# Sliding-window attention on one Trainium2 core: the next head's projection, cut in 32 pieces, is spread otherwise over the stages of a head

## The reference, cut to what matters

```
q = rope(x @ w_q[group, head])            # three groups: 3 projections per head
for (window, dilation) in ((128, 1), (512, 4), (2048, 16)):
    o_g, lse_g = dilated_window_attention(q_g, k_g, v_g, window, dilation)
wts = softmax(stack(lse_g), axis=0)       # over the three groups, for each token
o = sum(wts * o_g);  y = (o * silu(x @ w_z[head])) @ w_out
```

## Time and profile before

| what | us |
| --- | --- |
| median of 3 runs | 3097.6 |
| lowest and highest | 3094.42 and 3098.24 |
| the profiled execution, its own time | 3098.63 |
| its span, first to last instruction | 3096.8 |
| TensorE busy in it | 2830.1 |

### The profile page before, as it was taken

One profiled execution on the slowest core, in us unless ns is written; L12 is line 12 of the kernel. 1 busy time (PEld: TensorE's weight loads), 2 busy tenths in 40 slices (PEclk: granted clock), 3 DMA queues, 4 the chain that ended last, 5 costly groups with the idle time before them and its releaser, 6 DMA issues. The chain is left out here.

```text
span 3096.8 us, 38843 instructions
## 1 busy us (share of the span) xinstructions
PE 2830.1 (91%) x14702; PEld 2317.9 (75%) x14702; DVE 1544.5 (50%) x1992; ACT 1185.0 (38%) x1974; POOL 965.6 (31%) x490
## 2 busy tenths in 40 slices
PE   6989887989999999979689999999789988999988
PEld 5777765868888888867377777777567777888876
DVE  5765755541444234446735666656644215444443
ACT  4122223232444334442525545555533315434331
POOL 3543533235333453323043333333031331000020
PEclk9999999989999999989899999999989998999999
DMA  4213330311100110103121111111032110000021
GB/s 150 89 54 102 109 101 28 135 62 41 35 28 28 35 42 28 30 19 129 48 57 28 41 42 35 41 42 35 14 102 75 41 48 14 15 8 14 8 89 55
DMA packets 57305, 162.33 MB, mean 52 GB/s; under 512 B 8400, under 2 KB 10064, under 8 KB 57168
## 3 DMA queue, kind: packets, MB, share of 16 engines
q1 hardware_dynamic: 49968, 134.17, 13.5%
q10 hardware_dynamic: 7200, 26.22, 2.5%
HBM read 133.99 MB, written 17.99 MB: 49 GB/s over the span
## 5 line engine op out<-in xcount | busy, mean ns | idle before, releaser
L108 POOL TENSOR_SCALAR w_hi<-w_raw 128x1024 fp32r<-128x1024 f32 x126 | 141.7, 1125 | 1533.2 <-PE pj L134 553.1
L110 POOL TENSOR_TENSOR w_lo<-w_raw,w_hi 128x1024 fp32r<-128x1024 f32 x126 | 308.3, 2447 | 19.0 <-issue 5.2
L1256 PE MATMUL pj<-x_hi,w_hi 128*128 128x512 f32 x688 | 286.3, 416 | 4.8 <-ACT swa_swapped L1387 4.8
L1258 PE MATMUL pj<-x_hi,w_lo 128*128 128x512 f32 x688 | 271.5, 395 | 0.0
L1257 PE MATMUL pj<-x_lo,w_hi 128*128 128x512 f32 x688 | 271.2, 394 | 0.0
L132 PE MATMUL pj<-x_hi,w_hi 128*128 128x512 f32 x544 | 220.7, 406 | 11.5 <-DVE gate_cumsum L548 7.5
L1707 PE MATMUL pj<-x_hi,w_hi 128*128 128x512 f32 x496 | 216.3, 436 | 7.4 <-ACT da_raw L1822 7.4
L133 PE MATMUL pj<-x_lo,w_hi 128*128 128x512 f32 x544 | 214.3, 394 | 0.0
L134 PE MATMUL pj<-x_hi,w_lo 128*128 128x512 f32 x544 | 213.9, 393 | 0.0
L1709 PE MATMUL pj<-x_hi,w_lo 128*128 128x512 f32 x496 | 195.8, 395 | 0.0
L1708 PE MATMUL pj<-x_lo,w_hi 128*128 128x512 f32 x496 | 194.7, 393 | 0.0
(11 more groups left out here) (353 smaller groups left out, 6674.9 us busy)
## 6 DMA issues: line engine op xcount, KB each, us to landing
w_raw<-w_slots SPq DMA_DIRECT2D x158, 512.0 KB, 3.5
o_t<-ada_t ACTq DMA_DIRECT2D x24, 512.0 KB, 3.6
ada_row<-ada_t ACTq DMA_DIRECT2D x24, 512.0 KB, 3.5
x_res<-o_t SPq DMA_DIRECT2D x24, 512.0 KB, 2.7
o_t<-x_res SPq DMA_DIRECT2D x24, 512.0 KB, 6.3
da_swapped<-da_raw SPq DMA_DIRECT2D x64, 128.0 KB, 2.3
o_t<-x_t SPq DMA_DIRECT2D x4, 1024.0 KB, 9.1
o_t<-x_t SPq DMA_DIRECT2D x8, 512.0 KB, 6.7
```

The source lines that it names most:

```text
L110: nc.gpsimd.tensor_tensor(g.w_lo[:, u, :], g.w_raw[:, u, :], g.w_hi[:, u, :], ALU.subtract)\
L1256: nc.tensor.matmul(proj(half), g.w_hi[:, u, w], g.x_hi[:, k, cols[half]], start=(k == 0), stop=False)
L1258: mm = nc.tensor.matmul(proj(half), g.w_lo[:, u, w], g.x_hi[:, k, cols[half]], start=False, stop=(k == KT - 1))
```

## The change

Only the order of work within a head of the sliding-window part changes; no computation is added or taken away. The pieces with the scores become one per step (10 in place of 16), ahead of the log-sums' transpose 6 in place of 4, between the two transposes 11 in place of 8, after the totals' transpose 2 in place of 2 (numbers 27 and 28 in place of 28 and 29), and 3 in place of 2 among the p steps. The calls that empty the banks follow on ScalarE and VectorE. On GpSimd the wait for `total_ready` moves from ahead of split(z+4) to ahead of rope(0). SyncE's program is unchanged.

```diff
-        WITH_SCORES = (0, 2, 4, 6, 8, 10, 11, 12, 14, 15, 16)
-        FIRST_T, COVER, FILL = 20, 28, 30
+        WITH_SCORES = range(N + 1)
+        FIRST_T, COVER, FILL = 16, 27, 29
...
                 if nxt:
                     for j in range(G):
-                        if j == 1:
+                        split_slot(nc, pool, g, s0 + z + 3 + j, hh * 4)
+                        if j == 0:
                             pool.wait_ge(m.total_ready, h + 1)
-                        split_slot(nc, pool, g, s0 + z + 3 + j, hh * 4)
-                        if j == 1:
+                        elif j == 1:
                             pool.wait_ge(m.p_ready, h * N + N)
                         rope(nxt, j, nz + j)
...
-                    if nxt and i in (2, 4):
-                        gate(i // 4)
-                    if i == 7:
-                        take(0, 0)
+                    if nxt and i in (4, 8):
+                        gate(i // 8)
...
                 nc.scalar.activation(spread(lse[:, :]), dense(den[:, :]), ACT.Ln).then_inc(m.ln_ready, 1)
-                take(0, 1)
+                take(0, 0)
                 act.wait_ge(m.lt_done, h + 1)
                 nc.scalar.copy(lse_t[:, :], turn(0)[0:96, 0:P]).then_inc(m.lt_ready, 1)
                 if not nxt:
                     gate(0)
-                take(1, 0)
+                take(0, 1)
...
                 nc.scalar.activation(ee[:, :, :], ee[:, :, :], ACT.Exp).then_inc(m.terms_exp, 1)
                 if not nxt:
                     gate(1)
...
                 nc.scalar.activation(ee[:, 0, :], ee[:, 0, :], ACT.Ln).then_inc(m.z_ln, 1)
+                take(1, 0)
                 take(1, 1)
-                take(2, 0)
...
                 nc.scalar.activation(dense(fac[:, :]), spread(lse[:, :]), ACT.Exp, scale=-1.0).then_inc(m.fac_ready, 1)
...
                     take_p(i)
-                    if i == 2:
-                        take(2, 1)
+                    if i in (1, 4):
+                        take(2, i // 4)
...
-                    if nxt and i in (3, 5):
-                        gate(i // 5)
-                    if i == 7:
-                        turn_q(0, 0)
+                    if nxt and i in (5, 9):
+                        gate(i // 9)
...
                 nc.vector.tensor_tensor(spread(lse[:, :]), spread(lse[:, :]), dense(nm[:, :]), ALU.subtract).then_inc(m.lse_ready, 1)
                 if not nxt:
                     gate(0)
+                turn_q(0, 0)
                 turn_q(0, 1)
-                turn_q(1, 0)
...
                 nc.vector.tensor_tensor(in_order(ee[:, 2, :], d2), by_token(nat[:, 1, :], d2), in_order(top[:, :], d2), ALU.subtract)\
                     .then_inc(m.terms_ready, 1)
+                turn_q(1, 0)
                 dve.wait_ge(m.terms_exp, h + 1)
...
                 nc.vector.tensor_tensor(by_token(total[:, 2, :], d2), in_order(ee[:, 0, :], d2), in_order(top[:, :], d2), ALU.add)\
                     .then_inc(m.total_ready, 1)
                 turn_q(1, 1)
-                turn_q(2, 0)
...
                 nc.vector.tensor_tensor(spread(lse[:, :]), spread(turn(1)[:, 0:96]), dense(nm[:, :]), ALU.add).then_inc(m.f_ready, 1)
                 dve.wait_ge(m.fac_ready, h + 1)
...
                     normalize(i)
-                    if i == 4:
-                        turn_q(2, 1)
+                    if i in (2, 7):
+                        turn_q(2, i // 7)
```

## The result

| kernel | median, us | lowest to highest | runs |
| --- | --- | --- | --- |
| before | 3094.56 | 3089.73 to 3105.95 | 8 |
| changed | 3112.50 | 3106.12 to 3128.51 | 8 |

The ratio is 1.005, with a 95% interval of 1.0035 to 1.0066: the change makes the kernel slower by 11 to 20 us. Forecast were +13.5 us, 3111 (3100 to 3121).

The account below looks back on a forecast made before the run. Sliding-window heads were taken as bound by TensorE's pieces, fixed work and the wait at L1358 (28.0 us). Terms 6.7 - 0.2 + 0.7 + 6.3 = +13.5 gave 3111 us from a 3097.6 median, range 3100 to 3121.

Parts of the forecast that it names:

- The load ahead of the write: SyncE's load(z+1) at T+4.20 (T: start of L1355) delays the log-sums' write L1186 to T+4.5, 3.8 us later.
- The data of the load: The write's data come after the load's in the same queue: read at T+8.05, T being the start of L1355.
- the two ends: Bounds for the read's issue: 1.57 us from the write (T+6.1) and 3.95 from the load (T+8.15); T starts L1355.
- The first rival: On SyncE's queue, small packets pass the load: idle at piece 24 is 1.9 us, no drops, 3086; chance 0.08.
- The rest of the chain: After the read: maximum T+9.85, logarithm done T+13.9, TensorE idle 3.85 us at piece 24; T starts L1355.
- The scores: In the score steps, one piece per step is cover enough and moving the gate's calls has no cost.
- Behind L1358: One more piece interrupts small matmuls, 0.1 us a head, +0.7; GpSimd's split beside the p scaling taken as 0.
- The clock: Idles of 3.85 us on TensorE bring seven clock drops in place of three, 1.58 each: +6.3 us.
- The sum: Whole kernel: 6.7 - 0.2 + 0.7 + 6.3 = +13.5 us; from a median of 3097.6, forecast 3111.
- The cover: Between L1355 and L1358, 11 pieces (15.1 us) would cover the whole wait if the chain kept its 14.2.
- The second rival: Between L1355 and L1358, the load does not hold the write and the whole wait goes: 3073; chance 0.04.

Follow-up runs that it names:

- the first experiment: Changed kernel with SyncE issuing load(z+1) behind the two reads L1190 instead of ahead of the write L1186; 3069.46 us, ratio 0.9918 to the kernel before.
- the turned order on the kernel before: Kernel before with one edit: SyncE issues load(z+1) behind the reads L1190; 3097.4 us, ratio 1.0002.
- Filling the idle: Changed kernel with 12 more matmuls ahead of piece 24, whose result nobody reads; 3106.62 us, ratio 1.0037 to the kernel before.
- the ropes alone: Kernel before with only the change's GpSimd part, the wait for the totals ahead of rope(0) instead of split(z+4); 3110.08 us, ratio 1.0045.
- GpSimd's old order: Changed kernel with rope(0) put back right behind split(z+3), and split(z+4) behind the totals; 3112.44 us, ratio 1.0055 to the kernel before.
- the calls put back: Changed kernel with turn_q(1, 0) and take(1, 0) put back ahead of the terms; 3108.25 us, ratio 1.0034 to the kernel before.
- the data taken away: Changed kernel, SyncE's split wait kept ahead of the write but followed by only 4 KB; weights' load behind the reads L1190; 3090.99 us, ratio 0.9987 to before.

## Why the prediction was right

- **The load ahead of the write.** Load at T+4.20 forecast, T+4.19 measured; write T+4.5 forecast, T+4.63 measured. Shown as the cause by the first experiment.
- **The data of the load.** Of the two ends I took 3.85 from the load to the read; measured 3.79 (864.71 to 868.50), and 1.57 from the write without the data. The first rival, small packets that pass the load, is out. One case does not fit and I left it out: in the first head before, the load went out at 792.40 and the write at 794.32, as far apart as in the earlier trace rows, but the read came at 798.57, 4.25 behind the write. No run settles what held it; with the load out of the way it took 1.61 in that head (the turned order on the kernel before).
- **The rest of the chain.** Maximum T+9.85 forecast, T+9.74 measured; logarithm done T+13.9 forecast, T+13.67 measured. TensorE's idle at piece 24 was to be 3.85; it is 26.6/7 = 3.80.
- **The scores.** One piece a step is cover: no wait at a score step in the changed profile beyond what was there.
- **Behind L1358.** The first p block is held while the split runs: in the second head L1536 took 2.19 us (882.01 to 884.20) in place of 0.68, beside GpSimd's L110 (881.26 to 883.65). TensorE does not wait for it, so the 0 that I took stands. The stretch of 19.29 us is 20.89, and 1.38 of that is the piece: 0.2 more, 0.1 forecast.
- **The clock.** Seven drops for three, forecast and found; the drop falls on the three pieces ahead of L1358, as one of two places named. 1.58 each was about right in the head that it falls in: 5.82 less 4.13 for three pieces and 0.1 for the first matmul is 1.6 in the second head. Filling the idle gave back 1.3 a head.
- **The sum.** The part grew by 11.1 us in the profiled execution against 13.5; 0.8 of the difference lies behind the last L1355 (36.53 before, 35.74 now), the rest is spread over the heads, 0.2 each. The medians differ by 17.9, the ratio's interval says 11 to 20. Where the 7 us between 11.1 and 17.9 lie is not shown; the profiled execution of the changed kernel is its fastest run, that of the kernel before lies above its median. That 3111 came within 1.5 us of 3112.50 is partly luck: I started from a median of 3097.6 from three runs, which eight runs put at 3094.56, and so a growth taken 4.4 too small met a start taken 3.0 too high.
- **The cover** of 11 pieces was right in size: with the load out of the way they take 15.1 us and nothing idles. The second rival was priced at 3073 for that case; the kernel that does it, with the turned order, has 3069.46.

## What to carry to other kernels

When work is moved on one engine, look which transfers are released by its end and what is queued behind them on the issuing engine. Here a prefetch that nobody needed soon stood ahead of the small DMAs of a serial chain, and letting one projection end four pieces closer to that chain put the prefetch's wait and its data into it. Issue such a prefetch in a pause of the chain, here between its first read and the totals' write. And test a change with its parts together as well as one by one: of its parts on the kernel before, the ropes alone lost 0.45%, and the turned order alone showed no gain in the medians.

## What the runs showed of the hardware

A two-operand VectorE instruction of 8 x 128 elements took 0.38 us with GpSimd quiet and ended 0.24 us after GpSimd's rope when that was under way, whether it began 0.8 or 1.4 us ahead of the rope's end: it took 1.01 and 1.64. Two writes of 4 KB, issued 0.44 us behind a load of 512 KB from the same engine, took 3.2 to 3.5 us to the issue that waits for them in the seven heads of the changed kernel, and 1.57 with no load or only 4 KB ahead. And idles of 3.7 to 4.0 us of TensorE had a granted clock below 1 behind them in all seven heads of the changed kernel, idles of 3.5 to 4.3 in six of seven (GpSimd's old order), idles of 3.2 to 3.6 in four of six (the calls put back, where the seventh, of 2.67, had one too), idles of 2.4 to 2.6 in two of six before and, in two of seven, with the turned order on the kernel before, and idles of about 2.0 in none of seven (the data taken away).
